# Narrower products in the doubling levels of a recurrence scan

## The reference

```python
def rwkv7_scan(r, w, k, v, kk, bb, s0):
    def step(s, inp):
        rt, wt, kt, vt, kkt, bt = inp
        sa = jnp.einsum('bhvk,bhk->bhv', s, kkt)
        s = s * wt[:, :, None, :] - sa[..., None] * bt[:, :, None, :] + vt[..., None] * kt[:, :, None, :]
        return s, jnp.einsum('bhvk,bhk->bhv', s, rt)
    xs = tuple(jnp.moveaxis(z, 1, 0) for z in (r, w, k, v, kk, bb))
    s, y = lax.scan(step, s0, xs)
    return jnp.moveaxis(y, 0, 1), s
```

## Time and profile before

| | |
|---|---|
| median of three runs | 3096.59 us |
| span of the profiled execution | 3101.2 us |
| the profiled execution's own time | not given beside its span |
| TensorE matmuls busy | 2848.1 us, 92% |
| TensorE weight loads busy | 2651.8 us, 86% |
| VectorE busy | 1749.0 us, 56% |
| ScalarE busy | 1255.2 us, 40% |
| mean granted TensorE clock | 0.955 |

### The profile page before, as it was taken

How to read it: one execution, slowest core, us unless ns; L and a number is a source line. 1 busy time by engine, 2 the same in 40 slices (tenths; PEclk the granted TensorE clock), 3 DMA queues, 4 the chain that set the end, 5 groups by cost and what they waited for, 6 DMA issues and landing times. The chain is left out here.

```text
span 3101.2 us, 63944 instructions
## 1 busy us (share of the span) xinstructions
PE 2848.1 (92%) x25694; PEld 2651.8 (86%) x25694; DVE 1749.0 (56%) x2611; ACT 1255.2 (40%) x1755; POOL 521.7 (17%) x341
## 2 busy tenths in 40 slices
PE   7998989989989999899989988999798899998997
PEld 7998888877788998799989978987787888977997
DVE  4444764586676665544354457545766766655443
ACT  4534631244332443444254355222543234434542
POOL 0003550054310000000000046400543000000000
PEclk9999989999998999899999999999999999999998
DMA  4444350144374566344344443401454664663443
GB/s 160 150 147 145 109 152 18 29 124 172 98 300 144 180 209 220 130 149 148 116 148 149 147 136 114 130 25 30 127 188 124 251 214 142 220 220 113 149 147 105
DMA packets 119694, 448.21 MB, mean 145 GB/s; under 512 B 13648, under 2 KB 23920, under 8 KB 111664
## 3 DMA queue, kind: packets, MB, share of 16 engines
q1 hardware_dynamic: 97920, 329.78, 33.4%
q0 software_dynamic: 21552, 115.34, 10.1%
HBM read 397.04 MB, written 48.02 MB: 144 GB/s over the span
## 5 line engine op out<-in xcount | busy, mean ns | idle before, releaser
L1531 ACT ACTIVATE w_high<-ring 128x1024 fp32r<-128x1024 f32 x598 | 631.9, 1057 | 746.9 <-PE gemm_banks L901 315.7
L897 PE MATMUL gemm_banks<-in_high,w_high 128*128 128x320 f32 (+1 forms) x2720 | 803.3, 311 | 25.5 <-ACT w_high L1531 13.9
L1944 DVE TENSOR_TENSOR w_low<-ring,w_high 128x1024 fp32r<-128x1024 f32 x436 | 532.5, 1222 | 472.7 <-ACT w_high L1531 472.3
L898 PE MATMUL gemm_banks<-in_low,w_high 128*128 128x320 f32 (+1 forms) x2720 | 795.4, 308 | 0.0
L732 POOL TENSOR_TENSOR w_low<-ring,w_high 128x1024 fp32r<-128x1024 f32 x162 | 414.3, 2566 | 970.9 <-ACT w_high L1531 969.7
L897 PEld LDWEIGHTS gemm_banks<-in_high,w_high 128*128 128x128 f32 x2720 | 515.1, 189 | 32.4 <-issue 14.0
L898 PEld LDWEIGHTS gemm_banks<-in_low,w_high 128*128 128x128 f32 x2720 | 514.9, 189 | 1.7
L901 PE MATMUL gemm_banks<-in_high,w_low 128*128 128x320 f32 (+1 forms) x2720 | 450.8, 308 | 6.3 <-POOL w_low L732 3.8
L901 PEld LDWEIGHTS gemm_banks<-in_high,w_low 128*128 128x128 f32 x2720 | 408.8, 189 | 8.7 <-POOL w_low L732 5.3
L946 PE MATMUL gemm_banks<-in_high,w_high 128*128 128x320 f32 x640 | 208.9, 339 | 22.1 <-DVE arena L2070 16.7
L973 PE MATMUL gemm_banks<-act_high,w_high 128*128 128x320 f32 x704 | 208.2, 308 | 2.5 <-DVE arena L1993 2.5
(11 more groups left out here) (420 smaller groups left out, 4237.4 us busy)
## 6 DMA issues: line engine op xcount, KB each, us to landing
ring<-in_w SPq DMA_DIRECT2D x598, 512.0 KB, 3.6
arena<-in_kc POOLq DMA_DIRECT2D x14, 1024.0 KB, 6.5
arena<-in_vc POOLq DMA_DIRECT2D x14, 1024.0 KB, 7.3
out_fill<-stage SPq DMA_DIRECT2D x80, 160.0 KB, 4.0
arena<-in_ssm POOLq DMA_DIRECT2D x16, 512.0 KB, 13.5
out_s_ssm<-arena POOLq DMA_DIRECT2D x16, 512.0 KB, 13.9
arena<-in_ret POOLq DMA_DIRECT2D x16, 512.0 KB, 22.2
out_s_ret<-arena POOLq DMA_DIRECT2D x16, 512.0 KB, 7.0
```

The lines of the kernel that those rows point to most:

```text
L897: mm(dst, w_high[:, slot, w(k)], in_high[:, k, 0:n], start=(k == 0), stop=False)
L898: mm(dst, w_high[:, slot, w(k)], in_low[:, k, 0:n], start=False, stop=False)
L1531: f(w_high[:, slot], ring[:, s, 0:D], ACT.Copy).then_inc(weights_high, 1)
L1944: tt(w_low[:, slot], ring[:, pos % RING, 0:D], w_high[:, slot].bitcast(F32), ALU.subtract).then_inc(weights_split, 1)
```

## The change

The products of a level move half of the columns: those of the odd blocks for `ux` and for the first product of `xy`, those of the even blocks for the second. They go to the same places in the banks as before. The other columns of these places are no longer written in these steps, and no instruction reads them. No mark, wait or step is moved, and the VectorE program is as it was.

```diff
+                def blocks(v, b, half):
+
+                    return v.rearrange("p (a two b) -> p a two b", two=2, b=b)[:, :, half, :]
+
...
-                            each_pair(g, ("ux", m), lambda p, q: heads(view(g, 3, 0)[:, q], Lc[:, p], Xc[p]))
+                            each_pair(g, ("ux", m), lambda p, q: heads(
+                                blocks(view(g, 3, 0)[:, q], 1 << m, 1), Lc[:, p], blocks(Xc[p], 1 << m, 1)))
                         for g in GROUPS:
                             need(V, (c, ("y", m), g))
 
                             def xy(p, q):
-                                Y = Ys[:, m - 1, p]
-                                ins_ = heads(view(g, 2, 0)[:, q], XTc[p], Y)
+                                Y, b = Ys[:, m - 1, p], 1 << m
+                                ins_ = heads(blocks(view(g, 2, 0)[:, q], b, 1), XTc[p], blocks(Y, b, 1))
                                 if m < levels_of(c)[-1]:
-                                    ins_ = heads(view(g, 2, 256)[:, q], Y, XTc[p])
+                                    ins_ = heads(blocks(view(g, 2, 256)[:, q], b, 0), Y, blocks(XTc[p], b, 0))
                                 return ins_
                             each_pair(g, ("xy", m), xy)
```

## The result

The changed kernel takes 3143.64 us (median of four runs, 3141.52 to 3156.3), the kernel before 3095.64 us in the same comparison. The ratio is 1.0158, with a 95% interval of 1.014 to 1.0176: slower by 48 us. Forecast were 3143 us.

A forecast was written before the change was run, and what follows sets the result against it. TensorE was taken to bound the kernel, busy 92% of the span, with VectorE's answers short between. Terms 44 + 4 - 1 = 47 us on the 3096.6 us median gave about 3143 us, range 3105 to 3167.

The forecast's parts named there:

- Records do not get cheaper with 32 columns: TensorE level products: pace stays about 29 ns per record, as in the 16-column read; priced 0, at best 57 us saved.
- Rival 2: Narrowed level records come faster than 29 ns, half of 57 us gained: 3068 us; chance 0.04.
- The clock falls in the level stretch, in levels 1 to 2: Scan levels: narrow products halve the TensorE clock in most chunks, until full-width products bring it back; forecast chance 0.76.
- the term of the prompt chunks: Scan's prompt chunks: 304 records at half clock, 24 ns more each, in six of eight chunks: 44 us.
- The 24 ns per record: TensorE records in the scan: extra time of each at half clock, 53 ns against 29 ns at full clock.
- The term of the sample chunks: Levels 1 and 2 ahead of the read: about 80 more records at half clock, 2 us per layer, 4 us.
- The sum: Whole kernel: 44 + 4 - 1 = 47 us slower, put on the median: about 3143 us.
- The tail: End of each level's TensorE burst: 25 ns earlier with 32 columns fewer; 1 us saved, between 0 and 2.2.
- the first (clock stays): Scan levels keep the full clock, only burst ends get shorter: 3095.6 us, no measurable change; chance 0.12.
- the third (strided runs): Levels 1 and 2: runs of 2 or 4 elements double record time, 28 or 54 us: 3125 to 3150 us; chance 0.08.
- the Trainium skill's advice on gaps: TensorE clock falls when the PE idles between bursts; the change makes no gap, so it would cost nothing.

## Why the prediction was right

- **Records do not get cheaper with 32 columns**: right. 1.13 us for 32 records at both widths at full clock. Rival 2 is refuted.
- **The clock falls in the level stretch, in levels 1 to 2**: right, and shown as the cause by three comparisons: all columns in the same order restore the time, narrowing only where full-width products stand between costs nothing, and widening the read gains.
- **Its price**: the term of the prompt chunks was 44 us. The sample chunk's levels stand ahead of the read, so the windows up to the read hold them too; cut where VectorE begins the sample chunk's first `y`, the prompt chunks before and after the change are:

```profile
455.40:578.30 122.90, 110.28 (x3793) 104.44 (x3792) 59.52 (x137) 29.31 (x87) 9.92 (x10) 0.99 0.11 28
1991.60:2113.60 122.00, 109.15 (x3793) 103.22 (x3792) 59.49 (x137) 29.29 (x87) 9.92 (x10) 1.00 0.11 28
...
454.10:597.10 143.00, 132.00 (x3793) 127.45 (x3792) 59.45 (x136) 29.26 (x86) 9.94 (x10) 0.80 0.09 24
2009.50:2154.60 145.10, 133.95 (x3793) 129.45 (x3792) 59.46 (x137) 29.32 (x87) 9.85 (x10) 0.79 0.09 23
```

  They grew by 20.1 + 23.1 = 43 us. It came about otherwise than the step said: not six of eight chunks with half of their records, but all eight, with some 255 to 324 records each and not 304, at 43 / 8 = 5.4 us a chunk and not 7.3. That the two errors cancel is luck. The 24 ns per record was right: 32 records take 1.95 us, less a tail of about 0.3 that is 53 ns each. But at half clock no wait or tail of a level is left: it repeats every 5.12 us (500.36 to 505.48) against 3.14, which is 1.98 us more and not 96 x 24 ns = 2.3. The term of the sample chunks was 4 us and too small: the rest of the scans grew by 24.8 - 20.1 = 4.7 us in layer 1 and 25.2 - 23.1 = 2.1 in layer 2. In layer 1 the clock is at half for 27.3 us there, where it was for 13.7 before.
- **The sum**: 47 us forecast, 48 measured between the medians. The two scans grew by 24.8 + 25.2 = 50 us in the profiles, the spans by 38.8 only: outside the scans the changed kernel's profiled execution is 11 us shorter, with the same instructions. Half of that lies between the two scans, and the clock goes with it:

```profile
602.90:1991.60 1388.70, 1290.27 (x8493) 1200.12 (x8493) 808.78 (x1149) 591.54 (x777) 250.36 (x158) 0.95 0.48 157
626.40:2009.50 1383.10, 1283.08 (x8497) 1191.39 (x8497) 809.07 (x1149) 591.61 (x777) 250.41 (x158) 0.96 0.48 158
```

  The change does not touch this part, and the kernel before spreads by 30 us from run to run by itself, mostly with its mean clock (0.952 to 0.963). So these 11 us are a difference between two executions, and that the sum meets the median to 1 us is luck too.
- **The tail**: wrong in its place. The step took 0.8 ns per column from the durations at 64 and 128 columns, and let each burst end 25 ns earlier. At full clock a narrowed record has the same duration as a wide one:

```profile
L1056 PE MATMUL gemm_banks<-arena 64*64 64x32 f32 x32 | 1.3, 219 | 0.0
```

  Against it stand 219 ns at 64 columns and 269 at 128. What is shorter is the beginning of a burst that starts from a wait:

```profile
496.01 0.65 PE L1056 MATMUL gemm_banks<-arena 64*64 64x32 f32 x16 [1.31 <-DVE arena L2177]
```

  With 64 columns the same burst takes 0.68 us. These 0.03 us in each of 44 levels would be about 1 us at full clock, as much as the term; the runs can't tell so little from nothing, and many levels of the changed kernel run at half clock.
- **Rivals**: the first (clock stays) fell with the clock row; the third (strided runs) with the kernel that moves all columns in short runs. The Trainium skill's sentence on non-contiguous PSUM access ("SBUF — State Buffer", Door 1) finds no support here for runs of two fp32 values: 1.13 us per burst with and without them. And the Trainium skill's advice on gaps ("TensorE: Matmul & The Clock Gate", "Why this matters for your kernels") would have given no change: the trace has the clock at half with TensorE busy for 13.53 of 13.60 us.
- **What the prediction overlooked**: waits may have a part in it. Before the fall at 498.0 TensorE is busy for 2.62 of 4.40 us (first row of the table around the chunk), with a wait of 1.31 us; the kernel before has that wait too (1.29 us) and keeps its clock. But in the first chunk of layer 1, where TensorE waits longer, the clock of the kernel before falls in level 1 with 64 columns, for 3.4 us:

```profile
459.70:463.10 3.40, 1.56 (x50) 1.45 (x51) 2.73 (x6) 0.38 (x1) 0.00 (x0) 1.00 0.04 13
463.10:466.50 3.40, 3.40 (x71) 3.40 (x69) 1.41 (x3) 0.00 (x0) 0.00 (x0) 0.50 0.00 0
```

  The products were narrowed with the waits left as they are, so it is shown that fewer columns bring the clock down in this stream; whether they would without the waits of level 1 was not tried. The read, where the clock falls with no wait inside it, speaks for it.

## What to carry to other kernels

Before moving fewer columns through TensorE, look whether the pace of its records follows the columns at all; if it does not, as here from 16 to 64, there is nothing to gain and the clock to lose. Then look in the same trace for the thinnest dense work and the granted clock there: in this case the read showed beforehand what the clock would do. Where thin work can't be avoided, wider products that compute columns nobody reads may be faster, as the read shows.

## What the runs showed of the hardware that I had not expected

- The cost of thin work does not go evenly with the columns: 48 of 64 columns cost at most 0.34%, 32 of 64 cost 1.4 to 1.8%, and the same narrowing in levels 3 to 5, between full-width products, costs nothing.
- With 32 weight columns in turn over four places a record comes every 8 to 9 ns, but not for long: after 180 records TensorE stands idle for 2.38 us, waiting for nothing that the profile shows ("issue" in the timeline above). That its instructions arrive too slowly is a guess, not shown. Cutting the products made the records three times as fast, and the read's half no shorter: its second group begins 4.9 us after the first.
